# Native fp32 scores for the paired heads of a hybrid attention layer, with their copies and the output-weight split moved between engines

## Chip, cores and metric

The kernel runs on one core of a Trainium2 chip. The metric is device microseconds of one execution, the median over several runs. The engines are called PE (TensorE; PEld is its weight load), DVE (VectorE), ACT (ScalarE), POOL (GpSimd) and SP (SyncE, which issues the DMAs).

## What is computed

One decoder layer on x (512 tokens, width 1024), all fp32: a pre-norm and one input projection; eight latent-attention heads (0 to 7, query width 96); eight block-sparse heads (8 to 15, width 64, which with 512 tokens amount to causal attention with rotated queries and keys); the 16 head outputs together go through one output projection `w_out`, post-norm and residual; then a squared-ReLU MLP with the same norms. The part that matters here:

```python
mla_o = mla_attention(c_q, c_kv, k_r, ...)                      # heads 0 to 7
moba_o = moba_attention(rope(q), rope(k), v)                    # heads 8 to 15, scale 64 ** -0.5
mix = jnp.concatenate([mla_o..., moba_o...], axis=-1)
h = h + rms_norm(mix @ w_out[l], attn_post_g[l])
u = rms_norm(h, mlp_pre_g[l])
a = jnp.square(jax.nn.relu(u @ w_up[l]))
h = h + rms_norm(a @ w_down[l], mlp_post_g[l])
```

## The kernel before, in words

**Split products.** Most products are made at near-fp32 accuracy from three passes of the type fp32r: each operand is split into a high part (ACT, `hi_part`, L562) and a low part, the whole minus the high part (DVE, `lo_part`, L882; POOL for some pieces, L501), and PE makes high*high, high*low and low*high (`mm3`, L1329 to L1331). The weighted sums of values (`weighted`, L1556) are made in native fp32 with one matmul call per head and key tile, each of which stands as two records in the trace. Transposes are matmuls against an identity.

**Heads.** Queries stand in four tiles t of 128 tokens; tile t needs keys 0 to 128(t+1). Heads 0 to 7 are worked one by one. Heads 8 to 15 are worked in pairs m = 4 to 7 (`FIRST` = 4, `NP` = 8), one head in the upper and one in the lower 64 rows of PE's array. A turn m on PE is: scores of pair m for tiles 3, 2, 0 (`pair_scores`, L1497); what is left of the transposes of the last pair; transposes of the probabilities of head a = 2m-2 (`probs_T`, L1535); the weighted sums of pair m-2; scores of tile 1; the last transposes of a, those of head b = 2m-1; and, for m = 4 and 5, the transposes of keys and queries of pair m+2 (`k_prep` L1460, `q_prep` L1441). After the last turn come weighted sums of pair 6, transposes of head 14, one output tile of chunk 0 (`out_early(0)`, 12 products), transposes of head 15, one output tile of chunk 1 (`out_early(1)`), weighted sums of pair 7, then the other tiles of chunks 0 and 1 (72 products), then chunks 2 and 3.

**The other engines in a turn.** DVE takes row maxima (L996), ACT makes exponentials and their sums (L654), DVE inverts the sums (L1023), POOL multiplies the probabilities by them (`norm`, L508), PE transposes them into banks 3, 4 and 5, and ACT (`p_part`, L682) or DVE (L1045) copy these to SBUF, each bank having to be copied before it is used again (`p3_ready`, `p4_ready`, `p5_ready`). Queries and keys of a pair are split from their bank by ACT then DVE (`q_part`, `k_part`). Every engine works in the order written out by hand; semaphores tie them together. The scores of pair m wait for all exponentials of pair m-1 (`s_exp`).

**Output weights.** `w_out` comes in four chunks of 1 MB. SP loads chunks 0 and 1 early, chunk 2 once the split of chunk 0 is complete (`wo_ready` at 1), chunk 3 once that of chunk 1 is (`wo_ready` at 2). Chunks 0 and 1 are split in eight pieces of 512 columns, high part by ACT, low part by POOL (`out_piece`). `OUT_PIECES` and `PAIR_PIECES` say behind which turn each piece is made: piece 0 after head 6, piece 1 with turn 4, piece 2 with turn 5, pieces 3 and 4 with turn 6, 5 and 6 with turn 7, piece 7 after that. On POOL the pieces of a turn stand behind its norms, that is behind the eight `norm` calls of that turn. Chunks 2 and 3 (pieces 8 to 15) are split by ACT and DVE after the last weighted sum.

Of the kernel before, what the change touches and what calls it, by code (L numbers as in the profile page):

```python
# [23 lines left out]
P = 128  # L24
# [8 lines left out]
def build(nc, x, attn_pre_g, w_in, mla_q_norm_g, w_mla_q_up, mla_kv_norm_g, w_mla_kv_up, w_out,  # L33
# [42 lines left out]
    with ExitStack() as ctx:  # L76
# [126 lines left out]
        qT_full, qh, ql = sem("qT_full"), sem("qh"), sem("ql")  # L203
        kT_full, kh, kl = sem("kT_full"), sem("kh"), sem("kl")
        s_full, s_nb, s_exp = sem("s_full"), sem("s_nb"), sem("s_exp")
        s_ri, s_norm = sem("s_ri"), sem("s_norm")
# [36 lines left out]


        def by_head(w):
            return w[:, 0:HEADS * P].rearrange("p (h k c) -> p h k c", h=HEADS, k=2)
# [201 lines left out]
        def _(pool):  # L448
# [62 lines left out]
            for i in range(HEADS):  # L511
                for n in OUT_PIECES.get(i - 1, []):
# [33 lines left out]
        def _(act):  # L546
# [89 lines left out]
            def q_part(i):  # L636
                if prepared(i):
                    act.wait_ge(qT_full, preps(i))
                    if before(i) >= 0:
                        act.wait_ge(s_full, 3 * (before(i) + 1))  # L640
                    rows = QH if i < HEADS else P
                    hi_part(qT_hi[slot(i)][0:rows, :], ps[q_bank(i)][0:rows, :]).then_inc(qh, 1)

            def k_part(i):
                if prepared(i):
# [3 lines left out]
                    r0, rows = (NOPE * (i % 2), NOPE) if i < HEADS else (0, P)  # L649
                    hi_part(kT_hi[slot(i)][0:rows, :], ps[k_bank(i)][r0:r0 + rows, :]).then_inc(kh, 1)  # L650

# [59 lines left out]
            for i in range(1, HEADS - 1):  # L711
                if i >= 2:
                    p_part(i - 1, 0)
                if i <= 4:
                    k_part(i + 2)
                if i == 5:
                    o_part(0)
                for n in OUT_PIECES.get(i, []):
                    out_piece(n)
                if i >= 2:  # L720
                    p_part(i - 1, 2)
                exps(i + 1, S_ORDER[:1])
                if i == 6:
                    k_part(HEADS + 2)
                q_part(i + 2)
                exps(i + 1, S_ORDER[1:])
                if i in (4, 5):
                    k_part(i + 3)

            for m in range(FIRST, NP):  # L730
# [19 lines left out]
                for n in PAIR_PIECES[m]:  # L750
                    out_piece(n)
            p_part(NH - 2, 0)
            o_part(NP - 2)
            for n in PAIR_PIECES[NP]:
                out_piece(n)
            p_part(NH - 2, 2)
            p_part(NH - 1, 0)
# [115 lines left out]
        def _(dve):  # L873
# [151 lines left out]
            def q_part(i):  # L1025
                if prepared(i):
                    dve.wait_ge(qh, preps(i))
                    rows = QH if i < HEADS else P
                    s = slot(i)
                    lo_part(qT_lo[s][0:rows, :], ps[q_bank(i)][0:rows, :], qT_hi[s][0:rows, :]).then_inc(ql, 1)  # L1030

            def k_part(i):
                if prepared(i):
                    dve.wait_ge(kh, preps(i))
                    r0, rows = (NOPE * (i % 2), NOPE) if i < HEADS else (0, P)
                    s = slot(i)
                    lo_part(kT_lo[s][0:rows, :], ps[k_bank(i)][r0:r0 + rows, :], kT_hi[s][0:rows, :]).then_inc(kl, 1)

# [25 lines left out]
            def out_piece(n):  # L1064

                per = CW // PIECE
                c, w = n // per, slice(PIECE * (n % per), PIECE * (n % per) + PIECE)
                dve.wait_ge(wo_hi_ready, n + 1)
                last = lo_part(wo_lo[c - 2][:, w], raw[c % 2][:, w], wo_hi[c - 2][:, w])
                if n % per == per - 1:  # L1070
                    last.then_inc(wo_ready, 1)
# [18 lines left out]
            for m in range(FIRST, NP):  # L1090
# [235 lines left out]
        def _(pe):  # L1326
# [98 lines left out]
            def q_prep(i):  # L1425
                if prepared(i):
# [17 lines left out]
            def k_prep(i):  # L1444

                if i % 2 == 0 and i < NH:
                    b = k_bank(i)
                    if i in (2, 4):
                        pe.wait_ge(v_ready, NT + (3 if i == 2 else 4))
                    elif i > HEADS + 2:  # L1450
                        pe.wait_ge(p5_ready, i - 5)
                    elif i > 4:
                        pe.wait_ge(kl, i if i <= HEADS else preps(i) - 1)
                    if i < HEADS:
# [24 lines left out]
            def pair_scores(m, tiles):  # L1479

                s = slot(2 * m)
                if 3 in tiles:
                    pe.wait_ge(kl, preps(2 * m))
                    pe.wait_ge(ql, preps(2 * m))
                for t in tiles:
                    if t == 3:
                        pe.wait_ge(s_exp, 2 * NT * m)
                    if t == 2 and m == FIRST:
                        pe.wait_ge(kl, preps(HEADS + 2))
# [28 lines left out]
            def probs_T(i, tiles):  # L1518
                if tiles[0] == 0:
                    pe.wait_ge(s_norm, NT * (i + 1) + (1 if i >= HEADS and i % 2 == 0 else 0))  # L1520
                for k in tiles:
# [8 lines left out]
                    if k == 2 and i == HEADS - 2:  # L1530
                        pe.wait_ge(ql, preps(HEADS + 2))
                    if k == 2 and i in (HEADS - 1, HEADS + 1):
                        pe.wait_ge(kl, preps(i + 5))
                    for t in range(k, NT):
# [5 lines left out]
            def weighted(m, tiles):  # L1540

                if 0 in tiles:
# [3 lines left out]
                    if m in (FIRST - 1, FIRST):  # L1546
                        pe.wait_ge(ql, preps(HEADS + 4) + m - (FIRST - 1))
                for k in tiles:
# [52 lines left out]
            for m in range(FIRST, NP):  # L1601
# [23 lines left out]
            for c in range(2):  # L1625
                for t in range(1, NT):
                    if c == 0 and t == NT - 1:
                        pe.wait_ge(ol, NH // 2)
                    last = out_tile(t, c)
                last.then_inc(w_used, 1)  # L1630
            pe.wait_ge(wo_ready, NO)
# [123 lines left out]
```

## Time and profile before

| | |
|---|---|
| median of 3 runs | 566.77 us (565.98 to 567.16) |
| the profiled execution | 567.1 us, its span 565.3 us |
| PE busy | 550.5 us, 97% of the span |
| DVE, ACT, POOL busy | 391.9, 297.3, 95.4 us |
| mean granted TensorE clock | 0.998 |

Times inside the trace are microseconds from the start of the span. The profiled execution's own time is 1.8 us above its span. The input projection fills the span to about 100 us, the heads and pairs to about 188, the output projection to about 236, the MLP the rest.

### The profile page before, as it was taken

What the parts mean: (1) busy time and instruction counts of PE and PEld (TensorE: products, weight loads), DVE (VectorE), ACT (ScalarE), POOL (GpSimd) and SP (SyncE); (2) the same over time, 40 slices, a digit from 0 to 9 for tenths busy, and PEclk for the clock granted to TensorE, in tenths of its full rate; (3) what the DMA queues carried; (4) which work ended last, traced back from release to release, by engine and by line L of the source; (5) the groups of instructions that cost most, each with busy time, mean ns of one, the idle gap of its engine ahead of it and who ended that gap; (6) DMA issues with size and microseconds to landing.
All of it is one profiled execution on the core that took longest, in us unless ns stands there. A gap on an engine that the chain in (4) does not pass through costs nothing.

```text
span 565.3 us, 7927 instructions
## 1 busy us (share of the span) xinstructions
PE 550.5 (97%) x2776; PEld 457.7 (81%) x2776; DVE 391.9 (69%) x750; ACT 297.3 (53%) x624; POOL 95.4 (17%) x157
## 2 busy tenths in 40 slices
PE   7999999999999999999999999999999999999994
PEld 7988898877666788998888888888888888888883
DVE  5349563488875446457775776579868889787897
ACT  6563172688886354445335334435454657556461
POOL 1253210355779002200000000000000001000003
PEclk9999999999999999999999999999999999999999
DMA  8921522000002750078767888687984555606403
GB/s 293 375 84 57 176 85 75 0 2 2 0 2 78 277 188 18 26 294 301 272 225 277 273 272 288 226 282 278 346 301 173 215 181 193 217 14 215 150 0 149
DMA packets 41774, 97.23 MB, mean 172 GB/s; under 512 B 2192, under 2 KB 20368, under 8 KB 38416
## 3 DMA queue, kind: packets, MB, share of 16 engines
q1 hardware_dynamic: 41312, 96.32, 48.9%
q10 hardware_dynamic: 432, 0.53, 0.3%
q8 instruction: 17, 0.28, 0.2%
q14 instruction: 13, 0.11, 0.1%
HBM read 81.11 MB, written 15.73 MB: 171 GB/s over the span
## 4 chain that ended last, share of the span: by engine, by line
PE 93%; ACT 2%; DVE 2%; issue 1%; DMA 1%; POOLq 0%; DVEq 0%; POOL 0%; ACTq 0%
PE bank L1329 27%; PE bank L1331 27%; PE bank L1330 27%; PE bank L1357 4%; PE bank L1535 2%; PE bank L1556 2%; PE bank L1497 1%; ACT probs L654 1%; DVE bank L996 1%; DMA g_in<-in_attn_pre_g 1%; PE bank L1441 1%; PE bank L1335 1%; ACT pT L682 0%; DVE pT L1045 0%; PE bank L1396 0%
## 5 line engine op out<-in xcount | busy, mean ns | idle before, releaser
L1329 PE MATMUL bank<-uT_hi,w_hi 128*128 128x512 f32 (+1 forms) x280 | 104.1, 372 | 0.0
L1330 PE MATMUL bank<-uT_lo,w_hi 128*128 128x512 f32 (+1 forms) x280 | 103.8, 371 | 0.0
L1331 PE MATMUL bank<-uT_hi,w_lo 128*128 128x512 f32 (+1 forms) x280 | 103.8, 371 | 0.0
L1329 PE MATMUL bank<-w_hi,a_hi 128*128 128x512 f32 x224 | 87.2, 389 | 0.0
L1330 PE MATMUL bank<-w_lo,a_hi 128*128 128x512 f32 x224 | 87.1, 389 | 0.0
L1331 PE MATMUL bank<-w_hi,a_lo 128*128 128x512 f32 x224 | 87.1, 389 | 0.0
L885 DVE SCALAR_TENSOR_TENSOR w_lo<-w_raw,g_up,w_hi 128x256 fp32r<-128x256 f32 x128 | 52.1, 479 | 47.5 <-ACT w_hi L562 47.5
L562 ACT ACTIVATE w_hi<-w_raw,g_up 128x256 fp32r<-128x256 f32 x128 | 53.0, 496 | 44.8 <-PE bank L1331 25.0
L562 ACT ACTIVATE w_hi<-w_raw 128x1024 fp32r<-128x1024 f32 (+2 forms) x49 | 46.8, 1001 | 52.4 <-PE bank L1331 48.8
L882 DVE TENSOR_TENSOR w_lo<-w_raw,w_hi 128x1024 fp32r<-128x1024 f32 (+1 forms) x41 | 49.0, 1234 | 22.2 <-ACT w_hi L562 22.1
L1331 PEld LDWEIGHTS bank<-uT_hi,w_lo 128*128 128x128 f32 x280 | 52.7, 188 | 9.1
L1330 PEld LDWEIGHTS bank<-uT_lo,w_hi 128*128 128x128 f32 x280 | 52.7, 188 | 9.0
L1329 PEld LDWEIGHTS bank<-uT_hi,w_hi 128*128 128x128 f32 x280 | 52.7, 188 | 9.0
L508 POOL TENSOR_TENSOR probs<-probs,rs 128x512 f32<-128x512 f32 (+3 forms) x64 | 44.1, 723 | 54.1 <-DVE rs L1016 46.6
L1329 PE MATMUL bank<-w_hi,uT_hi 128*128 128x512 f32 x128 | 50.3, 393 | 0.0
L1331 PE MATMUL bank<-w_hi,uT_lo 128*128 128x512 f32 x128 | 49.9, 390 | 0.0
L1330 PE MATMUL bank<-w_lo,uT_hi 128*128 128x512 f32 x128 | 49.8, 389 | 0.0
L1329 PEld LDWEIGHTS bank<-w_hi,a_hi 128*128 128x128 f32 x224 | 42.0, 188 | 9.0 <-issue 0.4
L1331 PEld LDWEIGHTS bank<-w_hi,a_lo 128*128 128x128 f32 x224 | 42.0, 188 | 8.8
L1330 PEld LDWEIGHTS bank<-w_lo,a_hi 128*128 128x128 f32 x224 | 42.0, 188 | 8.8
L824 ACT ACTIVATE act_sb<-relu 128x512 f32 (+1 forms) x32 | 20.0, 624 | 51.1 <-DVE relu L1188 51.1
L538 POOL TENSOR_TENSOR relu<-relu,post_g 128x512 f32<-128x512 f32 x2 | 2.7, 1396 | 230.9 <-ACT junk_down L590 230.9
(163 smaller groups left out, 975.7 us busy)
## 6 DMA issues: line engine op xcount, KB each, us to landing
stage<-in_w_down SPq DMA_DIRECT2D x17, 1024.0 KB, 4.9
w_raw<-in_w_up SPq DMA_DIRECT2D x16, 1024.0 KB, 8.4
pair_sums<-stage SPq DMA_DIRECT2D x13, 1024.0 KB, 9.9
w_raw<-in_w_down SPq DMA_DIRECT2D x10, 1024.0 KB, 6.5
w_raw<-pair_sums SPq DMA_DIRECT2D x10, 1024.0 KB, 4.8
w_raw<-in_w_in SPq DMA_DIRECT2D x6, 1024.0 KB, 6.9
w_raw<-in_w_out SPq DMA_DIRECT2D x4, 1024.0 KB, 4.8
stage<-pair_sums SPq DMA_DIRECT2D x3, 1024.0 KB, 4.8
```

The lines of the kernel that those rows point to most:

```text
L508: nc.gpsimd.tensor_tensor(pr, pr, rs[:, i % 4, t:t + 1].to_broadcast([P, P * (t + 1)]), ALU.mult).then_inc(s_norm, 1)
L562: return nc.scalar.activation(out, whole, ACT.Copy, scale=scale)
L654: nc.scalar.activation(probs[i % 4][:, p_off(t):p_off(t) + n], ps[b][:, c:c + n], ACT.Exp, bias=nb[:, i % 4, t:t + 1], scale=-1.0, accum_o ...
L824: nc.scalar.activation(act_sb[:, bass.ds(i * 4 + tile, 1), :], relu[:, tile % 2:tile % 2 + 1, :], ACT.Square).then_inc(a_ready, 1)
L882: return nc.vector.tensor_tensor(out, whole, hi.bitcast(F32), ALU.subtract)
L885: return nc.vector.scalar_tensor_tensor(out=out, in0=whole, scalar=scale, in1=hi.bitcast(F32), op0=ALU.mult, op1=ALU.subtract)
L1329: nc.tensor.matmul(out, lh, rh, start=start, stop=False)
L1330: nc.tensor.matmul(out, lh, rl, start=False, stop=False)
L1331: return nc.tensor.matmul(out, ll, rh, start=False, stop=stop)
L1357: last = nc.tensor.matmul(ps[t][:, 0:CA], x[:, k, P * t:P * t + P], h[s][:, w], start=k == 0 and n == 0, stop=k == ND - 1 and n == 2)
L1535: last = nc.tensor.transpose(ps[b][:, c + P * (t - k):c + P * (t - k) + P], probs[i % 4][:, p_off(t) + P * k:p_off(t) + P * k + P], ident[ ...
L1556: last = nc.tensor.matmul(ps[6][r0:r0 + VD, P * k:TOP], v_sb[:, i // HEADS, k, vc], pT[i % 4][:, w], start=k == 0, stop=k == NT - 1)
```

## The change

- Queries and keys of heads 8 to 15 are copied whole, in fp32, from their bank to new tiles `mqT` and `mkT` by DVE alone (semaphores `mq_ready`, `mk_ready`); ACT has no part in them. The third copies of the four fp32r tiles go.
- `pair_scores` makes one native fp32 matmul call per head and tile where it made three fp32r ones.
- The third copy of the transposed probabilities (bank 5, 256 columns) of heads 6, 8, 10, 12 and 14 goes from ACT to DVE, right behind the last maxima of a turn.
- POOL makes only pieces 0 to 3 (one behind each turn 4 to 7); DVE makes pieces 4 to 7, behind the copies of head 15.
- On PE, the tile of chunk 0 is moved ahead of the last transposes and weighted sums but one; the early tile of chunk 1 goes, and in its place stand 12 products of chunk 0 (`SPARE`). All of chunk 1 comes after all of chunk 0.

```diff
-        for name, tiles in (("qT_hi", qT_hi), ("qT_lo", qT_lo), ("kT_hi", kT_hi), ("kT_lo", kT_lo)):
-            tiles.append(sb(f"{name}2", [P, S], F32R, stack=att))
+        mqT, mkT = [[sb(f"{n}{i}", [P, S], stack=att) for i in range(3)] for n in ("mqT", "mkT")]
...
         def ACT_COPIES(i, n):
-            return n == 0 or n == 2 and (i < HEADS or i % 2 == 0 or i in (HEADS - 1, HEADS + 1))
+            return n == 0 or n == 2 and (i < HEADS - 2 or i in (HEADS - 1, HEADS + 1))
...
-        OUT_PIECES = {6: [0]}
-        PAIR_PIECES = {4: [1], 5: [2], 6: [3, 4], 7: [5, 6], 8: [7]}
+        PAIR_PIECES = {4: [0], 5: [1], 6: [2], 7: [3], 8: [4, 5, 6, 7]}
...
@@ gpsimd @@
-            for n in PAIR_PIECES[NP]:
-                out_piece(n)
...
@@ scalar @@
-                pair_exps(m, [6])
-                p_part(a, 2)
-                pair_exps(m, [7])
+                pair_exps(m, [6, 7])
...
+            for n in PAIR_PIECES[NP]:
+                out_piece(n)
             p_part(NH - 2, 0)
             o_part(NP - 2)
-            for n in PAIR_PIECES[NP]:
-                out_piece(n)
-            p_part(NH - 2, 2)
             p_part(NH - 1, 0)
...
@@ vector @@
             def q_part(i):
-                if prepared(i):
+                if i >= HEADS:
+                    dve.wait_ge(qT_full, preps(i))
+                    if before(i) >= 0:
+                        dve.wait_ge(s_full, 3 * (before(i) + 1))
+                    nc.vector.tensor_copy(whole_q(i), ps[q_bank(i)][:, :]).then_inc(mq_ready, 1)
...
                 pair_maxes(m, [6, 7])
+                p_part(a, 2)
                 o_part(m - 2)
...
             p_part(NH - 2, 1)
+            p_part(NH - 2, 2)
             o_part(NP - 2)
             p_part(NH - 1, 1)
             p_part(NH - 1, 2)
+            dve.wait_ge(wo_ready, 1)
+            for n in PAIR_PIECES[NP]:
+                out_piece(n)
             o_part(NP - 1)
...
@@ tensor @@
-                    elif i == HEADS + 2:
-                        pe.wait_ge(ql, preps(HEADS))
+                    elif i == HEADS + 2:
+                        pe.wait_ge(mq_ready, 1)
...
-                    for n, (q, k) in enumerate(((qT_hi, kT_hi), (qT_hi, kT_lo), (qT_lo, kT_hi))):
-                        for h in range(2):
-                            b, c = PAIR_AT[t][h]
-                            r = slice(MOBA_D * h, MOBA_D * h + MOBA_D)
-                            last = nc.tensor.matmul(ps[b][:, c:c + w], q[s][r, tok], k[s][r, 0:w], start=n == 0, stop=n == 2)
-                            if n == 2 and t != 2:
-                                last.then_inc(s_full, 1)
+                    for h in range(2):
+                        b, c = PAIR_AT[t][h]
+                        r = slice(MOBA_D * h, MOBA_D * h + MOBA_D)
+                        last = nc.tensor.matmul(ps[b][:, c:c + w], whole_q(2 * m)[r, tok], whole_k(2 * m)[r, 0:w],
+                                                start=True, stop=True)
+                        if t != 2:
+                            last.then_inc(s_full, 1)
...
-            def out_early(c):
+            def out_ready(c):
 
                 pe.wait_ge(wo_ready, c + 1)
                 pe.wait_ge(s_exp, NT * NH)
                 pe.wait_ge(ol, 2 * (c + 1))
-                out_tile(0, c)
+
+            SPARE = ((1, 0), (3, 1))
...
+            out_ready(0)
+            out_tile(0, 0)
+            probs_T(NH - 2, PT_ORDER)
             weighted(NP - 2, range(NT))
-            probs_T(NH - 2, PT_ORDER)
-            out_early(0)
             probs_T(NH - 1, PT_ORDER)
-            out_early(1)
+            for t, b in SPARE:
+                for kk in range(2):
+                    out_rows(t, b, 0, kk)
             weighted(NP - 1, range(NT))
```

## Rows read from the trace of the kernel before

**Rows 1.** The page: the chain that ended last, by engine.

```profile
PE 93%; ACT 2%; DVE 2%; issue 1%; DMA 1%; POOLq 0%; DVEq 0%; POOL 0%; ACTq 0%
```

**Rows 2.** Timeline of PE, turns 4 to 7: start, us, what [idle before, releaser].

```profile
137.42 0.65 PE L1460 MATMUL bank<-ident,mk_nat 128*128 128x128 f32 x4 [0.32 <-DVE kT_lo L882]
...
142.11 0.50 PE L1497 MATMUL bank<-kT_hi,qT_hi 64*128 64x512 f32 x2 [0.93 <-ACT probs L654]
...
149.69 0.66 PE L1460 MATMUL bank<-ident,mk_nat 128*128 128x128 f32 x4 [0.25 <-ACT pT L682]
...
158.45 0.66 PE L1460 MATMUL bank<-ident,mk_nat 128*128 128x128 f32 x4 [0.62 <-ACT pT L682]
...
167.22 0.44 PE L1535 MATMUL bank<-ident,probs 128*128 128x128 f32 x2 [0.64 <-ACT pT L682]
...
174.87 0.44 PE L1535 MATMUL bank<-ident,probs 128*128 128x128 f32 x2 [0.20 <-ACT pT L682]
175.81 2.37 PE L1556 MATMUL bank<-pT,v_sb 128*64 128x512 f32 x16 [0.51 <-ACT pT L682]
```

**Rows 3.** Windows: us, PE, PEld, DVE, ACT, POOL busy, clock, DMA.

```profile
176.00:188.30 12.30, 12.30 (x77) 8.49 (x75) 2.38 (x4) 3.26 (x7) 6.46 (x8) 1.00 0.28 97
```

**Rows 4.** Timeline of PE: scores of pair 5 and what follows them.

```profile
150.71 0.50 PE L1497 MATMUL bank<-kT_hi,qT_hi 64*128 64x512 f32 x2
...
151.04 0.39 PE L1497 MATMUL bank<-kT_lo,qT_hi 64*128 64x512 f32 x2
...
151.27 0.40 PE L1497 MATMUL bank<-kT_hi,qT_lo 64*128 64x512 f32 x2
...
152.42 1.31 PE L1535 MATMUL bank<-ident,probs 128*128 128x128 f32 x10
...
155.97 0.39 PE L1497 MATMUL bank<-kT_hi,qT_hi 64*128 64x256 f32 x2
...
156.52 1.31 PE L1535 MATMUL bank<-ident,probs 128*128 128x128 f32 x10
```

**Rows 5.** Groups by form, 128 to 190 us: busy, mean ns, idle before.

```profile
L1045 DVE COPY pT<-bank 128x512 f32<-128x512 f32 x12 | 8.1, 676 | 5.9 <-PE bank L1535 5.9
...
L562 ACT ACTIVATE kT_hi<-bank 128x512 fp32r<-128x512 f32 x4 | 2.5, 632 | 0.0
```

**Rows 6.** Timeline of DVE at the end of turn 7.

```profile
174.80 0.17 DVE L1023 RECIPROCAL rs<-rs 128x3 f32<-128x3 f32 x1
...
175.54 0.40 DVE L1045 COPY pT<-bank 128x256 f32<-128x256 f32 x1
```

**Rows 7.** Timeline of POOL, turns 6 and 7: norms (L508) and pieces (L501).

```profile
167.33 3.48 POOL L508 TENSOR_TENSOR probs<-probs,rs 128x256 f32<-128x256 f32 x6 [1.35 <-DVE rs L1023]
170.77 2.52 POOL L501 TENSOR_TENSOR w_lo<-w_raw,w_hi 128x512 fp32r<-128x512 f32 x2
173.22 5.49 POOL L508 TENSOR_TENSOR probs<-probs,rs 128x512 f32<-128x512 f32 x8
```

**Rows 8.** Timeline of SP, PE and DVE: chunk loads, first product after weighting, late pieces.

```profile
172.08 10.77 SPq L342 DMA_DIRECT2D w_raw<-in_w_out  x2
...
188.26 0.50 PE L1329 MATMUL bank<-w_hi,uT_hi 128*128 128x512 f32 x1
...
189.62 4.90 DVE L882 TENSOR_TENSOR wo_lo<-w_raw,wo_hi 128x512 fp32r<-128x512 f32 x8
```

**Rows 9.** Windows at the end; PE at the start: timeline, groups 3:9.5 and 10.5:25.

```profile
558.30:562.80 4.50, 0.00 (x0) 0.00 (x0) 4.02 (x6) 0.72 (x2) 2.08 (x4) 1.00 0.31 118
562.80:565.30 2.50, 0.00 (x0) 0.00 (x0) 0.08 (x1) 0.00 (x0) 0.00 (x0) 0.50 0.54 210
...
5.85 1.76 PE L1357 MATMUL bank<-w_hi,uT_hi 128*128 128x416 f32 x4 [0.87 <-ACT w_hi L562]
...
L1357 PE MATMUL bank<-w_hi,uT_hi 128*128 128x416 f32 x4 | 1.8, 590 | 0.9 <-ACT w_hi L562 0.9
...
L1357 PE MATMUL bank<-w_hi,uT_hi 128*128 128x416 f32 x26 | 9.1, 351 | 0.0
```

More of the change, by code:

```diff
@@ L242, in before, with whole_q, whole_k @@
             return i - 2 if i < HEADS else SLOT_BEFORE.get(i, -1)
+        def whole_q(i):
+            return mqT[slot(i)][:, :]
+        def whole_k(i):
+            return mkT[slot(i)][:, :]
         def by_head(w):
@@ L511, in _ @@
             for i in range(HEADS):
-                for n in OUT_PIECES.get(i - 1, []):
-                    out_piece(n)
                 for n, t in enumerate(S_ORDER):
@@ L636, in q_part @@
             def q_part(i):
-                if prepared(i):
+                if i < HEADS:
                     act.wait_ge(qT_full, preps(i))
@@ L640, in q_part @@
                         act.wait_ge(s_full, 3 * (before(i) + 1))
-                    rows = QH if i < HEADS else P
-                    hi_part(qT_hi[slot(i)][0:rows, :], ps[q_bank(i)][0:rows, :]).then_inc(qh, 1)
+                    hi_part(qT_hi[slot(i)][0:QH, :], ps[q_bank(i)][0:QH, :]).then_inc(qh, 1)
             def k_part(i):
-                if prepared(i):
+                if i < HEADS:
                     act.wait_ge(kT_full, k_preps(i))
@@ L648, in k_part @@
                         act.wait_ge(s_full, 3 * (before(i) + 1))
-                    r0, rows = (NOPE * (i % 2), NOPE) if i < HEADS else (0, P)
-                    hi_part(kT_hi[slot(i)][0:rows, :], ps[k_bank(i)][r0:r0 + rows, :]).then_inc(kh, 1)
+                    r0 = NOPE * (i % 2)
+                    hi_part(kT_hi[slot(i)][0:NOPE, :], ps[k_bank(i)][r0:r0 + NOPE, :]).then_inc(kh, 1)
             def exp_tile(i, t, b, c):
@@ L717, in _ @@
                     o_part(0)
-                for n in OUT_PIECES.get(i, []):
-                    out_piece(n)
                 if i >= 2:
@@ L1025, in q_part @@
             def q_part(i):
-                if prepared(i):
+                if i >= HEADS:
[3 more added lines that the diff above has]
+                    nc.vector.tensor_copy(whole_q(i), ps[q_bank(i)][:, :]).then_inc(mq_ready, 1)
+                else:
                     dve.wait_ge(qh, preps(i))
-                    rows = QH if i < HEADS else P
                     s = slot(i)
-                    lo_part(qT_lo[s][0:rows, :], ps[q_bank(i)][0:rows, :], qT_hi[s][0:rows, :]).then_inc(ql, 1)
+                    lo_part(qT_lo[s][0:QH, :], ps[q_bank(i)][0:QH, :], qT_hi[s][0:QH, :]).then_inc(ql, 1)
             def k_part(i):
-                if prepared(i):
+                if i >= HEADS:
+                    dve.wait_ge(kT_full, k_preps(i))
+                    if before(i) >= 0:
+                        dve.wait_ge(s_full, 3 * (before(i) + 1))
+                    nc.vector.tensor_copy(whole_k(i), ps[k_bank(i)][:, :]).then_inc(mk_ready, 1)
+                else:
                     dve.wait_ge(kh, preps(i))
-                    r0, rows = (NOPE * (i % 2), NOPE) if i < HEADS else (0, P)
-                    s = slot(i)
-                    lo_part(kT_lo[s][0:rows, :], ps[k_bank(i)][r0:r0 + rows, :], kT_hi[s][0:rows, :]).then_inc(kl, 1)
+                    r0, s = NOPE * (i % 2), slot(i)
+                    lo_part(kT_lo[s][0:NOPE, :], ps[k_bank(i)][r0:r0 + NOPE, :], kT_hi[s][0:NOPE, :]).then_inc(kl, 1)
             def p_part(i, n):
@@ L1068, in out_piece @@
                 dve.wait_ge(wo_hi_ready, n + 1)
-                last = lo_part(wo_lo[c - 2][:, w], raw[c % 2][:, w], wo_hi[c - 2][:, w])
+                hi, lo = (w_hi[w_slot(OUT_CH[c])], w_lo[w_slot(OUT_CH[c])]) if c < 2 else (wo_hi[c - 2], wo_lo[c - 2])
+                last = lo_part(lo[:, w], raw[c % 2][:, w], hi[:, w])
                 if n % per == per - 1:
@@ L1451, in k_prep @@
                         pe.wait_ge(p5_ready, i - 5)
+                    elif i == HEADS + 2:
+                        pe.wait_ge(mk_ready, 1)
                     elif i > 4:
-                        pe.wait_ge(kl, i if i <= HEADS else preps(i) - 1)
+                        pe.wait_ge(kl, i)
                     if i < HEADS:
@@ L1479, in pair_scores @@
             def pair_scores(m, tiles):
-                s = slot(2 * m)
                 if 3 in tiles:
-                    pe.wait_ge(kl, preps(2 * m))
-                    pe.wait_ge(ql, preps(2 * m))
+                    pe.wait_ge(mk_ready, m - FIRST + 1)
+                    pe.wait_ge(mq_ready, m - FIRST + 1)
                 for t in tiles:
@@ L1617, in _ @@
                     probs_T(b, PT_ORDER[3:])
+            out_ready(0)
+            out_tile(0, 0)
+            probs_T(NH - 2, PT_ORDER)
             weighted(NP - 2, range(NT))
-            probs_T(NH - 2, PT_ORDER)
-            out_early(0)
             probs_T(NH - 1, PT_ORDER)
-            out_early(1)
+            for t, b in SPARE:
+                for kk in range(2):
+                    out_rows(t, b, 0, kk)
             weighted(NP - 1, range(NT))
[L1625 to L1630, printed above, removed]
+            for t in range(1, NT):
+                for b in range(2):
+                    if (t, b) not in SPARE:
+                        for kk in range(2):
+                            if t == NT - 1:
+                                pe.wait_ge(ol, NH // 2)
+                            last = out_rows(t, b, 0, kk)
+            last.then_inc(w_used, 1)
+            out_ready(1)
+            for t in range(NT):
+                last = out_tile(t, 1)
+            last.then_inc(w_used, 1)
             pe.wait_ge(wo_ready, NO)
```

10 lines of the change are left out of this document (5 added, 5 removed).

## The prediction

> **What bounds the kernel.** I read the chain of waits first: PE carries 93% of it [rows 1], so a microsecond saved on PE is a microsecond only where PE runs or waits on the chain. The change lies between about 137 and 205 us, so I read PE's timeline there and looked for the rows with idle time ahead. There are five of them before the last turn's exponentials are summed: 0.32, 0.93, 0.25, 0.62 and 0.64 us, together 2.76, and then 0.20 and 0.51 [rows 2]. All the rest is packed: PE alone sets the pace of a turn, with ACT as the engine it waits for in six of the seven. From 176.00 to 188.30 PE is busy for all of the 12.30 us [rows 3]. Last I read POOL, because the change makes PE wait for one of its products at a new place. POOL is far from busy over the whole kernel, but it is solidly filled in turn 7 [rows 7].
>
> **The scores.** Before, the first part of a pair's scores (tiles 3, 2, 0; 1024 columns for each head) takes 152.42 - 150.71 = 1.71 us, tile 1 (256 columns) 156.52 - 155.97 = 0.55, together 2.26 [rows 4]. A pass of 512 columns for both heads starts 0.23 after the last one (151.04 to 151.27), so the two heads, in two halves of the array's rows, run at the same time. No row shows native fp32 with the array halved by rows. The nearest one is the weighted sum: native fp32, two heads in two halves of the array's columns, the same 1280 columns for each head, 2.37 us (the row at 175.81 [rows 2]). From it the first part would be 2.37 * 1024/1280 = 1.90 and tile 1 0.47 plus a start of some 0.11 (the first pass, 150.71 to 151.04, is that much longer than the next), 0.58. That is 0.19 + 0.03 = 0.22 more a pair, 0.9 for four. Bounds: no change in cost (the weighted sum in one piece is within 0.11 of 2.26), and, if the halves take turns, 2.1 more a pair (rival B). I take 0.9, by the nearest row. The gain of going from three passes to one call is thus nothing: a native call costs about what three passes do.
>
> **The copies.** ACT loses kT_hi and qT_hi of four pairs, 0.63 each [rows 5]. DVE makes one copy of 0.68 where it made a low part of 0.69 (the row of the 512-column copy stands for it), and no longer waits for ACT first. So the wait of 0.32 for kT_lo goes, and in front of the first pair ACT makes no kT_hi and qT_hi between the exponentials of head 7, for which PE waits 0.93. DVE must still take the maxima and make both copies before pair 4 starts, so I take 1.0 of these 1.25 as gained. Bounds 0.7 and 1.25.
>
> **The bank-5 copy.** ACT made it between the last two exponentials of a turn, and PE waited for it: 0.25, 0.62, 0.64, 0.20. DVE now makes it right behind the last maxima. DVE's own copy of this size takes 0.40 [rows 6]. Followed through each turn: in turn 4 the copy still ends about when PE wants the bank, 0.1 gained; in turn 5 0.5 gained; in turn 6 the bank is free in time, but the scores of pair 7 wait for the last exponential of pair 6, 0.2 gained net. Late next there is ACT's last exponential. Queued on DVE behind the copy are the low part of the head outputs and the reciprocals of the last sums, for which POOL waits: they come 0.35 later than the gain of PE would have them.
> Sum of gains at the reciprocal of turn 7 (174.80 before [rows 6]): 1.0 + 0.1 + 0.5 + 0.2 - 0.9 - 0.35 = 0.55. Bounds -0.3 and 2.8 (all five waits gone, scores and copy at nothing).
>
> **The end of the pairs decides.** Piece 3, the last one of chunk 0, was made by POOL with turn 6: norms end and the two pieces 3 and 4 start at 170.77, and SP loads chunk 2 at 172.08, once piece 3 is through [rows 7, 8]. It now stands behind all norms of turn 7. In turn 6 the six norms behind the reciprocal take 170.77 - 167.33 = 3.44, a piece 2.52 / 2 = 1.26 [rows 7]. From the reciprocal at 174.80, 0.25 until POOL starts (the reciprocal's 0.17 and a little), 3.44 and 1.26: 179.75 with nothing gained, 179.2 with the 0.55. The earlier norms are no longer held up by a second piece (POOL started those of turn 7 only at 173.22), but those behind the last reciprocal are not early for it.
> PE is through with turn 7 at 174.87 + 0.44 = 175.3, or about 174.2 with its gains. Its next instruction is now the tile of chunk 0, which waits for `wo_ready` at 1. Behind this wait are queued the transposes of head 14 and the weighted sums of pair 6, which need only norms long done or done 1.3 earlier, and which before filled exactly this time. So PE stands still for about 5.0 us, from 174.2 to 179.2.
> The work behind is what it was: 24 products, twice ten transposes, two weighted sums. Before it ran from 175.81 to 188.26, 12.45 us. So 179.2 + 12.45 = 191.65, against 188.26: **3.4 us later**. Without any gain it would be 3.9.
>
> **What lies beside other work.** DVE's pieces 4 to 7 take 4 * 0.69 = 2.8 behind the copies of head 15; chunk 1 is wanted only behind the 24 remaining products of chunk 0, some 5.5 us after the last weighted sum, so they are hidden. Chunk 2 loads 7 us later (179 for 172), chunk 3 at about 190 for 182.4. A load took under 6 us; with 4.9 for DVE's eight late pieces [rows 8] the split is done near 200. PE wants it after 72 products, at 0.23 each 16.6 us, at 208. Hidden, by 8 us. The next loads of SP (x again, the first of `w_up`) stand behind chunk 3 and move with the rest; if that cover went, it would cost what chunk 3's 1 MB takes, some 3 us. POOL's last pieces, behind its norms, cost nothing before and nothing now. ACT's pieces 4 to 7 fall in PE's pause.
>
> **Sum.** 567.1 + 3.4 = 570.5 for the profiled execution. The median of before is 0.3 lower, 566.8, so **570.2** for the median. A measurement of this kernel can tell about 0.2%, 1.1 us, from no change.
>
> **Rivals.**
> A. *The pause lowers PE's clock.* [...] The pause I forecast is 5.0. At the start, PE took up work at 5.85 after a wait of 0.9; the same form of product took 590 ns up to 9.5 and 351 from 10.5 on [rows 9]. [...] Such a stretch costs about half of it, 2.0: 572.2 (1 to 3 us by when it falls). [...] Chance 0.34.
> [...]
> B. *The halves take turns in native fp32.* For: no row has this form. Against: the weighted sums overlap in native fp32, the scores overlap by rows in fp32r. Price 2.1 a pair, 8.5 for four, all ahead of the reciprocal: 579. Chance 0.05.
> C. *Not slower.* The place is the reciprocal of turn 7, which sets POOL's piece 3. If the turns get so much shorter that it comes 2.8 earlier, the loss is under 1.1; from 3.9 on it is none. All five waits gone with scores and copy at nothing give 2.76: 568.0. Were the native call also quicker than the three passes by 0.1 a pair: 567.6. For: ACT loses 0.63 twice a pair and 0.4 in each turn, and ACT is what PE waits for. Against: with those gone, PE's own work fills the turn, and POOL's norms follow the reciprocal in any case. Chance 0.08.
> D. *The change does less than it says,* the calls being run as fp32r all the same. The new tiles are plain fp32 like the weighted sums', so I give this nothing of its own; it would leave 3.4 - 0.9 = 2.5.
>
> **Chances.** Forecast (3.4 later, clock up) 0.45, 569.4 to 570.9 from the bounds above; A 0.34, 571.2 to 573.4; B 0.05; C 0.08; 0.08 for a loss in between or beyond by a late load. The range 569.0 to 573.8 takes in the first two. Slower by over 0.2% (over 567.9): 0.90; same 0.07; faster 0.03.
>
> **What would show it.** Right: PE idle some 5 us ahead of the first product of the output projection (L1329's first row behind turn 7), released by POOL's w_lo (L501), which ends near 179; the waits for ACT at L1460 and L1535 gone or under 0.2; the first part of the scores near 1.9 us with two records a call; ACT without kT_hi of pairs; 24 products and weighted sums packed behind. Wrong: a PE that goes on without a wait at about 175 (C), scores of 3 to 4 us (B), a granted clock under 1.00 between 175 and 190 (A). My sum is wrong in size if the reciprocal of turn 7 is off 174.3 by more than a microsecond.

## The result, and the profile after

| | before | changed |
|---|---|---|
| median (6 runs each) | 566.78 us | **572.52 us** (571.84 to 573.8) |
| ratio, 95% interval | | 1.0100 (1.0087 to 1.0114) |
| profiled execution, its span | 567.1, 565.3 us | 571.84, 570.0 us |
| mean granted clock | 0.998 | 0.99, in every one of the 6 runs |

The change is 5.7 us slower. That is inside the range of 569.0 to 573.8, but not at its point: it is rival A, forecast at 572.2, and not the likeliest case of 570.2. The profiled execution of the changed kernel was the fastest of its six, and that of the kernel before was 0.3 above its median, so the traces differ by less (571.84 - 567.1 = 4.7) than the medians do.

The chain of waits of the changed kernel (its page) answers to [rows 1]: PE has grown from 93% to 95%, and POOL, at nothing before, has 1%, which is its time under PE's pause.

```profile
PE 95%; POOL 1%; DVE 1%; DMA 1%; issue 0%; ACT 0%; POOLq 0%; DVEq 0%; ACTq 0%
```

PE's timeline in the turns (as in [rows 2] and [rows 4]):

```profile
132.29 0.60 PE L1469 MATMUL bank<-ident,mk_nat 128*128 128x128 f32 x4
...
136.26 0.60 PE L1469 MATMUL bank<-ident,mk_nat 128*128 128x128 f32 x4
...
140.23 2.00 PE L1504 MATMUL bank<-mkT,mqT 64*128 64x512 f32 x12 [0.27 <-DVE mqT L1023]
...
147.86 0.66 PE L1469 MATMUL bank<-ident,mk_nat 128*128 128x128 f32 x4
...
149.04 2.00 PE L1504 MATMUL bank<-mkT,mqT 64*128 64x512 f32 x12
150.97 1.31 PE L1543 MATMUL bank<-ident,probs 128*128 128x128 f32 x10
...
154.51 0.70 PE L1504 MATMUL bank<-mkT,mqT 64*128 64x256 f32 x4
155.15 1.31 PE L1543 MATMUL bank<-ident,probs 128*128 128x128 f32 x10
...
165.53 2.00 PE L1504 MATMUL bank<-mkT,mqT 64*128 64x512 f32 x12
```

All waits for ACT of 0.2 us and more are gone; one of 0.27 for DVE's copy of the queries is new. The first part of the scores takes 150.97 - 149.04 = 1.93 us (1.71 before), tile 1 0.64 (0.55 before), and the 12 and 4 records stand for two a call: it is native fp32, with both heads at the same time (one record of each head starts at 149.04, and 0.70 us later both are through).

A caution in reading the two traces side by side: at 132.29 the changed kernel does what the kernel before did at 132.97, and PE's instructions up to there are the same. Most of the difference stands already near the start, where PE's first products are slow for some microseconds in both traces (590 ns each for 351 later before [rows 9], 589 for 350 in the changed kernel's), and for less long in the changed kernel's: the first quick one starts at 10.04 before and at 9.41 after. It is not a gain of the change: the two traces of one kernel run twice reach this row at 132.65 and 133.14. So 0.68 us of every gain read off the clock of the trace is the two executions' own start. Below, stretches are counted from this row (the first transposes of keys in native form, L1460 before, L1469 after), and end at the first product behind the last weighted sum: 188.26 - 132.97 = 55.29 before, 193.02 - 132.29 = 60.73 after, **5.44 more**.

What follows turn 7, on PE, then DVE's reciprocal of turn 7 and what POOL does meanwhile (as in [rows 6, 7, 8]):

```profile
171.80 1.47 PE L1543 MATMUL bank<-ident,probs 128*128 128x128 f32 x10
178.28 0.79 PE L1336 MATMUL bank<-w_hi,uT_hi 128*128 128x512 f32 x1 [5.01 <-POOL w_lo L506]
178.87 0.63 PE L1337 MATMUL bank<-w_lo,uT_hi 128*128 128x512 f32 x1
...
183.21 1.25 PE L1543 MATMUL bank<-ident,probs 128*128 128x128 f32 x10
184.40 2.38 PE L1564 MATMUL bank<-pT,v_sb 128*64 128x512 f32 x16
...
190.72 2.37 PE L1564 MATMUL bank<-pT,v_sb 128*64 128x512 f32 x16
193.02 0.50 PE L1336 MATMUL bank<-w_hi,uT_hi 128*128 128x512 f32 x1
```

```profile
173.29 0.17 DVE L1016 RECIPROCAL rs<-rs 128x3 f32<-128x3 f32 x1
...
170.42 2.04 POOL L513 TENSOR_TENSOR probs<-probs,rs 128x512 f32<-128x512 f32 x2
173.53 3.47 POOL L513 TENSOR_TENSOR probs<-probs,rs 128x256 f32<-128x256 f32 x6 [1.07 <-DVE rs L1016]
176.96 1.26 POOL L506 TENSOR_TENSOR w_lo<-w_raw,w_hi 128x512 fp32r<-128x512 f32 x1
```

PE stands still for 5.01 us, released by POOL's piece 3. Then it works at another pace: 0.43 from product to product where it was 0.23. Windows of the same kernel (us, PE, PEld, DVE, ACT, POOL busy, clock, DMA):

```profile
174.00:175.00 1.00, 0.00 (x0) 0.00 (x0) 0.43 (x3) 1.00 (x3) 1.00 (x3) 1.00 0.00 0
175.00:176.00 1.00, 0.00 (x0) 0.00 (x0) 0.00 (x0) 1.00 (x3) 1.00 (x3) 0.98 0.00 0
176.00:177.00 1.00, 0.00 (x0) 0.00 (x0) 0.00 (x0) 0.25 (x1) 1.00 (x3) 0.50 0.00 0
...
178.30:183.20 4.90, 4.90 (x12) 3.81 (x13) 0.00 (x0) 0.00 (x0) 0.00 (x0) 0.54 0.57 215
```

The granted clock falls to 0.50 at 175.96, 2.7 us after PE's last transpose (171.80 + 1.47), and is up again near 182.8. The work behind the pause takes 193.02 - 178.28 = 14.74 us, where the forecast had 12.45 from [rows 2, 8], 2.29 more. Not all of this is the clock's: with the pause filled and the clock up (experiment 2) the same work takes 191.36 - 178.67 = 12.69, so 2.05 is for the clock and 0.24 for the new order.

### The profile page after: what moved, and what is told of

Its sections match the earlier page's. It is cut to its first block, busy times and chain, and to the rows that moved or that the text cites. A ratio compares the mean times of both kernels' runs of the same rounds, so it can differ in the third digit from the quotient of the medians.

```text
span 570.0 us, 7856 instructions
## 1 busy us (share of the span) xinstructions
PE 553.6 (97%) x2744; PEld 456.7 (80%) x2744; DVE 395.5 (69%) x759; ACT 293.4 (51%) x611; POOL 91.0 (16%) x153
## 4 chain that ended last, share of the span: by engine, by line
PE 95%; POOL 1%; DVE 1%; DMA 1%; issue 0%; ACT 0%; POOLq 0%; DVEq 0%; ACTq 0%
PE bank L1336 27%; PE bank L1337 27%; PE bank L1338 27%; PE bank L1364 3%; PE bank L1543 3%; PE bank L1564 3%; PE bank L1504 2%; POOL probs L513 1%; PE bank L1448 1%; DMA g_in<-in_attn_pre_g 1%; PE bank L1342 1%; DVE bank L989 0%; PE bank L1469 0%; PE bank L1403 0%; POOL w_lo L506 0%
## 5 line engine op out<-in xcount | busy, mean ns | idle before, releaser
L875 DVE TENSOR_TENSOR w_lo<-w_raw,w_hi 128x1024 fp32r<-128x1024 f32 (+2 forms) x45 | 51.4, 1185 | 22.4 <-ACT w_hi L561 22.2
L652 ACT ACTIVATE probs<-bank,nb 128x512 f32<-128x512 f32 (+3 forms) x64 | 33.3, 529 | 17.2 <-DVE nb L989 16.7
```

The costliest lines, as they stand in the source:

```text
L652: nc.scalar.activation(probs[i % 4][:, p_off(t):p_off(t) + n], ps[b][:, c:c + n], ACT.Exp, bias=nb[:, i % 4, t:t + 1], scale=-1.0, accum_o ...
L875: return nc.vector.tensor_tensor(out, whole, hi.bitcast(F32), ALU.subtract)
```

## Experiments

In all, ten kernels in twelve runs. The medians drift by up to a microsecond from one chip session to the next (before: 566.78 to 567.8), so ratios are taken against the kernel before in the same session. The stretch defined above, read in each trace, tells finer differences than the medians do; in the two kernels run twice it came out within 0.01 us. Each is read from one execution, so where the clock falls inside the stretch it holds for a fall as that execution had it.

| kernel | median, before beside it | ratio (95%) | stretch, against 55.29 |
|---|---|---|---|
| changed | 572.52, 566.78 | 1.0100 (1.0087 to 1.0114) | 60.73, +5.44 |
| scores' side alone | 566.29, 567.2 | 0.9983 (0.9974 to 0.9992) | 53.86, -1.43 |
| pieces and PE's end alone | 574.09, 567.2 | 1.0114 (1.0097 to 1.0131) | 61.90, +6.61 |
| pause filled | 570.34, 567.2 | 1.0063 (1.0049 to 1.0076) | 58.68, +3.39 |
| pause part filled | 572.36, 567.8 | 1.0076 (1.0062 to 1.0090) | 61.11, +5.82 |
| PE's order back | 567.65, 567.8 | 0.9997 (0.9987 to 1.0006) | 55.11, -0.18 |
| piece 3 in turn 6 | 565.69, 567.2 | 0.9979 (0.9970 to 0.9988) | 53.59, -1.70 |
| the same, again | 565.46, 567.45 | 0.9966 (0.9953 to 0.9978) | 53.60, -1.69 |
| bank-5 copy alone | 566.07, 567.8 | 0.9968 (0.9956 to 0.9980) | 54.25, -1.04 |
| the same, again | 566.57, 567.45 | 0.9983 (0.9974 to 0.9992) | 54.26, -1.03 |
| whole scores alone | 566.6, 567.8 | 0.9980 (0.9970 to 0.9989) | 54.38, -0.91 |
| split scores, piece 3 in turn 6 | 566.22, 567.45 | 0.9976 (0.9967 to 0.9985) | 53.95, -1.34 |
| one-pass scores | 563.46, 567.45 | 0.9929 (0.9916 to 0.9943) | 51.24, -4.05 |

**1. Which half of the change costs.** The scores' side alone is the changed kernel with this undone:

```diff
-        PAIR_PIECES = {4: [0], 5: [1], 6: [2], 7: [3], 8: [4, 5, 6, 7]}
+        OUT_PIECES = {6: [0]}
+        PAIR_PIECES = {4: [1], 5: [2], 6: [3, 4], 7: [5, 6], 8: [7]}
...
-            out_ready(0)
-            out_tile(0, 0)
-            probs_T(NH - 2, PT_ORDER)
             weighted(NP - 2, range(NT))
+            probs_T(NH - 2, PT_ORDER)
+            out_early(0)
```

> The changed kernel with pieces 0 to 7, their order on ACT and POOL, and PE's order behind turn 7 all as before; native scores, DVE copies and the bank-5 copies on DVE stay. Theory (the loss is PE's pause for piece 3 and the clock it costs; the scores' side is a gain): no pause over 1 us, clock 1.00, some 1.5 us faster than before, 565.3. Rival (native scores cost the time): slower than before, 568 or more.

The pieces and PE's end alone is the mirror of it: the kernel before, with those lines as in the change.

> The kernel before with only the pieces and PE's order behind turn 7 as in the change; the scores stay in fp32r, split by ACT and DVE. Theory: piece 3 ends near 179.8, PE pauses 4.5 us from 175.3, the clock falls for some 6.8 us and costs 2.1: 3.9 + 2.1 more than before, 572.8. Rival (native scores cost the time): about 567.

Measured: 0.9 us faster (566.29 against 567.2), and 6.9 slower (574.09). The second kernel's timeline of PE has all its old waits and the pause:

```profile
142.54 0.50 PE L1492 MATMUL bank<-kT_hi,qT_hi 64*128 64x512 f32 x2 [0.93 <-ACT probs L647]
...
158.86 0.66 PE L1455 MATMUL bank<-ident,mk_nat 128*128 128x128 f32 x4 [0.63 <-ACT pT L675]
...
175.27 0.44 PE L1530 MATMUL bank<-ident,probs 128*128 128x128 f32 x2 [0.19 <-ACT pT L675]
180.18 0.80 PE L1324 MATMUL bank<-w_hi,uT_hi 128*128 128x512 f32 x1 [4.47 <-POOL w_lo L500]
```

and its row of waits `PE bank L1324 <- POOL w_lo L500: 4.5, 1, 4.5`. So the loss is whole without any native score, and the scores' side is a gain. Both parts add up: in the stretch -1.43 + 6.61 = 5.18, where both together are 5.44. The theory stands, the rival (native scores cost the time) falls. The size was a little off: 1.5 us was expected of the first, 0.9 measured by the medians (0.5 to 1.5 by the interval), and 6.0 of the second, 6.9 measured. In its profiled execution the work behind the pause took 15.13 us, 0.39 more than in the changed kernel: the clock's share is not the same every time.

**2. The clock's share.** PE's pause is filled with small bf16 products whose results are never used:

```diff
+            pe.wait_ge(s_exp, NT * NH)
+            warm(80)
             out_ready(0)
             out_tile(0, 0)
```

> The changed kernel with 80 small bf16 products of the identity (results overwritten, never used) in PE's pause, some 4.4 us of the 5.0, behind the wait for the last exponentials. Theory (the fall of the clock costs 2.1 us of work behind the pause): clock stays 1.00 to the end, the first product of chunk 0 still starts within 0.3 us of 178.3, time 2.1 less than the change, 570.4. Rival (the clock costs nothing because the engines behind it set the pace): 572.5.

```profile
171.91 1.74 PE L1543 MATMUL bank<-ident,probs 128*128 128x128 f32 x12
173.61 4.64 PE L1393 MATMUL bank<-ident_b 128*128 128x128 bf16 x80
178.67 0.50 PE L1336 MATMUL bank<-w_hi,uT_hi 128*128 128x512 f32 x1 [0.42 <-POOL w_lo L506]
```

```profile
173.60:178.30 4.70, 4.65 (x81) 4.47 (x80) 1.21 (x5) 3.03 (x6) 4.38 (x7) 1.00 0.02 3
178.30:183.20 4.90, 4.53 (x24) 3.52 (x26) 0.49 (x1) 0.59 (x1) 0.32 (x1) 1.00 0.60 214
```

The first fence is PE's timeline of this kernel, the second its windows (us, PE, PEld, DVE, ACT, POOL busy, clock, DMA). The product of chunk 0 starts where it did (178.67 - 132.68 = 45.99 from the common row, against 178.28 - 132.29 = 45.99 in the changed kernel), the clock stays at 1.00, and in the same 4.9 us 24 products and transposes get done where there were 12. The stretch is 2.05 shorter than the change's (60.73 to 58.68). By ratios, 1.0063 for 1.0100, the gain is 2.1; by the medians, each against the kernel before beside it, it is 2.6. So the clock costs 2.1 to 2.6 us and the waiting itself the rest, 3.4 in the stretch, net of what the scores' side gains.

Then 24 such products instead of 80:

> As the filled pause, with 24 small products (results unused) in place of 80: PE works 1.4 us more and then stands still for about 3.5. Theory that any pause of over 2.7 us (the time from PE's last transpose to the fall in the changed kernel) lowers the clock: as the change, 572.5, clock 0.99. Rival, that more than the pause's length counts, and a pause under 4 us is let pass in some or all runs: 570.4, clock 1.00.

In the profiled execution PE stood still for 3.54 us and the clock fell all the same, in its windows 2.1 us after its last small product (173.91 + 1.51 = 175.42 to near 177.5):

```profile
177.00:177.50 0.50, 0.00 (x0) 0.00 (x0) 0.00 (x0) 0.00 (x0) 0.50 (x1) 1.00 0.00 0
177.50:179.00 1.50, 0.04 (x1) 0.04 (x1) 0.00 (x0) 0.00 (x0) 1.41 (x2) 0.51 0.00 0
```

But that execution was the slowest of the five (572.97), and the five do not agree. Their mean granted clocks are 0.99, 0.993, 0.995, 0.993 and 0.995, where the changed kernel has 0.99 six times. A mean of 0.995 over 570.5 us leaves at most 2 * 0.0055 * 570.5 = 6.3 us at the lower level (an estimate, with the rounding). In the traces the fall in the pause lasts 6.8 us, and the ends of the 14 traces have 2.0 to 5.3 us at the lower level. So in two of the five the fall in the pause was shorter, or did not come. The median of 572.36 looks like the first theory's, but the kernel before beside it was slow too (567.8): the ratio is 1.0076, between 1.0063 with the pause filled and 1.0100 for the change. Neither side holds as written: a pause of 3.5 us does not lower the clock in the same way every time. The pieces alone, with a pause of 4.5 us, have one such execution as well, clock 0.995 and 572.29 us, against 0.99 to 0.992 and 573.03 to 574.53 for the other four.

The ends of the kernels show the same. There the clock falls after PE's last instruction, but not after a fixed time. One kernel run twice (piece 3 in turn 6) ends its work on PE at 556.40 and at 556.74. Windows of its two traces, first and second run:

```profile
556.40:558.40 2.00, 0.00 (x1) 0.00 (x0) 1.93 (x3) 0.72 (x2) 1.03 (x3) 1.00 0.00 0
558.40:559.40 1.00, 0.00 (x0) 0.00 (x0) 0.78 (x2) 0.00 (x0) 0.92 (x2) 0.68 0.03 10
...
556.70:561.70 5.00, 0.04 (x1) 0.00 (x0) 4.12 (x6) 0.72 (x2) 2.18 (x4) 1.00 0.29 113
561.70:562.20 0.50, 0.00 (x0) 0.00 (x0) 0.00 (x0) 0.00 (x0) 0.00 (x0) 0.63 1.05 410
```

A mean of 0.68 over 1.00 us puts the first fall at 558.76, 2.4 us after PE's last instruction, and 0.63 over 0.50 us puts the second at 561.83, 5.1 us after it. Over the 14 traces of this document the time goes from 2.1 (the changed kernel, PE's order back, bank-5 copy alone) to 5.3 (whole scores alone), with 4.6 in the kernel before. What decides it in one execution stays open; the next experiment has a pause short enough that the clock stays up.

**3. The order on PE.** Pieces stay as in the change; PE's order is put back:

```diff
-            out_ready(0)
-            out_tile(0, 0)
-            probs_T(NH - 2, PT_ORDER)
             weighted(NP - 2, range(NT))
+            probs_T(NH - 2, PT_ORDER)
+            out_ready(0)
+            out_tile(0, 0)
```

> The changed kernel with its pieces as they are (piece 3 still behind POOL's norms of turn 7), but on PE the weighted sums of pair 6 and the transposes of head 14 are put back ahead of the wait for piece 3. Theory: 3.6 us of work fill the pause, which shrinks from 5.0 to about 1.4, and the clock stays at 1.00: 3.6 + 2.1 less than the change, 0.2 us more or less than before. Rival (the place of piece 3 costs in any order, for the loads and pieces behind it): still 2 us or more over before.

```profile
174.72 2.38 PE L1564 MATMUL bank<-pT,v_sb 128*64 128x512 f32 x16 [0.43 <-ACT pT L680]
177.03 1.31 PE L1543 MATMUL bank<-ident,probs 128*128 128x128 f32 x10
179.31 0.50 PE L1336 MATMUL bank<-w_hi,uT_hi 128*128 128x512 f32 x1 [0.98 <-POOL w_lo L506]
```

5.6 us come back in the stretch (60.73 to 55.11) and the kernel is even with the one before (0.9997): 3.6 us of work now fill the pause, 1.0 of it is left, 0.43 goes to another wait, and the clock stayed at 1.00 through it. The theory stands and the rival falls: the late piece itself, with all the loads behind it, costs nothing further.

**4. The place of piece 3.** One piece earlier on POOL, the change's order on PE:

```diff
-        PAIR_PIECES = {4: [0], 5: [1], 6: [2], 7: [3], 8: [4, 5, 6, 7]}
+        PAIR_PIECES = {4: [0], 5: [1], 6: [2, 3], 7: [], 8: [4, 5, 6, 7]}
```

> The changed kernel with piece 3 made in turn 6 (behind piece 2) and none in turn 7; all else as in the change. Theory: wo_ready at 1 comes near 172, PE goes on without a pause at 173.3, clock 1.00; the 5.0 of the pause and 2.1 of the clock go: 7.2 less than the change, 565.3, faster than before by 1.5. Rival (POOL's norms of turn 7, held up by the second piece, make a new wait at the transposes of head 14): 1 to 2 us less of it back, 566.5 to 567.5.

> The same kernel as the run with piece 3 in turn 6, again beside the two above: 1.5 us faster than before.

Both runs are faster than before, by 1.5 and 2.0 us (0.9979 and 0.9966), and 7.1 us less in the stretch than the change, where 7.2 was expected. POOL is now filled without a gap from turn 6's last norms to turn 7's:

```profile
169.53 2.51 POOL L506 TENSOR_TENSOR w_lo<-w_raw,w_hi 128x512 fp32r<-128x512 f32 x2
172.00 5.47 POOL L513 TENSOR_TENSOR probs<-probs,rs 128x512 f32<-128x512 f32 x8
```

and PE has no wait behind turn 7 at all: the tile of chunk 0 stands in front of the transposes and covers even the 0.5 us that PE waited before the weighted sums [rows 2]. The rival, a new wait for the norms of turn 7, did not come. One number in a table of the kernel decides between 1% slower and 0.2 to 0.3% faster.

**5. Where the gain of the scores' side comes from.** The bank-5 copy alone, in the kernel before:

```diff
-            return n == 0 or n == 2 and (i < HEADS or i % 2 == 0 or i in (HEADS - 1, HEADS + 1))
+            return n == 0 or n == 2 and (i < HEADS - 2 or i in (HEADS - 1, HEADS + 1))
...
-                pair_exps(m, [6])
-                p_part(a, 2)
-                pair_exps(m, [7])
+                pair_exps(m, [6, 7])
```

> The kernel before with only the 256-column copy of heads 6, 8, 10, 12 and 14 moved from ACT to DVE, behind the last maxima. Theory: PE's waits for ACT of 0.25, 0.62, 0.64 and 0.20 shrink to under 0.2 each, of which 0.5 to 1.0 us stays at the end: 0.1 to 0.2% faster. Rival (the waits were the queues' own and return elsewhere, as DVE's reciprocals come later): no gain.

> The same kernel as the run with the bank-5 copy alone, again beside the run with piece 3 in turn 6: its trace gained 1.0 us where that one gained 1.7, so by the traces it is the slower of the two by 0.7; by the medians so far it is even with it.

Gains of 0.32% and 0.17% by the medians, 1.04 us in the stretch. In its timeline the waits of 0.25, 0.62, 0.64 and 0.20 are gone, and one of 0.47 stands ahead of pair 7, for ACT's last exponential:

```profile
166.68 0.50 PE L1496 MATMUL bank<-kT_hi,qT_hi 64*128 64x512 f32 x2 [0.47 <-ACT probs L654]
```

Next, whole scores alone: the first kernel of experiment 1 with the bank-5 copies back on ACT, between the last two exponentials.

> The run of the scores' side alone, with the bank-5 copies back on ACT: only native scores and DVE's whole copies of queries and keys differ from before. Theory: 1.2 us gained ahead of pair 4 (the waits of 0.32 and 0.93), 0.3 lost to each pair's dearer scores, of which PE's waits for the bank-5 copy take up part: 0.3 to 0.8 us faster than before. Rival (the native calls are the gain): as fast as with the bank-5 copies moved too, 0.9 faster.

0.9 us in the stretch, 0.2% (1.1 us) by the ratio: somewhat more than the 0.3 to 0.8 expected. By the medians it can't be told from the run with the bank-5 copies moved too (0.9980 and 0.9983), which is the rival's figure; by the stretch it is behind that run by 0.5 (53.86 and 54.38). That the native calls themselves are the gain does not follow from it: they take 2.57 us a pair where the three passes take 2.26, and the waits ahead of pair 4 have gone from 1.25 to 0.27. The waits for ACT's bank-5 copy have shrunk to 0.20 each even without moving it. The two gains are therefore not additive (1.04 and 0.91 alone, 1.43 together): each shortens the same waits for ACT's copy.

Last, the price of native scores against split ones with everything else equal: the kernel before with the bank-5 copy on DVE, piece 3 in turn 6 and the change's order on PE.

> The kernel before with the bank-5 copies on DVE, piece 3 in turn 6 and the change's order behind turn 7; scores and their operands stay split in fp32r. Against the run with piece 3 in turn 6 and native scores this prices the native scores and whole copies by themselves. Theory: the waits of 0.32 and 0.93 stay, four pairs' scores are 0.3 cheaper each: even within 0.3 us of that run, 565.7 to 566. Rival (native scores are worth a microsecond or more): 567.

53.95 against 53.59 with native scores: native scores and whole copies are worth 0.36 us in the stretch. By the medians, 566.22 and 565.46 in the same session, 0.8, with intervals that overlap (0.9967 to 0.9985, 0.9953 to 0.9978). So they are worth a few tenths, a little more than the 0.3 that was expected at most, and no full microsecond is shown. With split scores PE's waits of 0.32, 0.93 and 0.48 stay in the turns, 1.46 more than the 0.27 with native scores, and this outweighs the cheaper passes (4 * 0.31 = 1.24).

**6. Does PE set the pace of a turn now?** The run of experiment 4 with its whole queries and keys in fp32r, one pass; the two low passes are left out.

```diff
-        mqT, mkT = [[sb(f"{n}{i}", [P, S], stack=att) for i in range(3)] for n in ("mqT", "mkT")]
+        mqT, mkT = [[sb(f"{n}{i}", [P, S], F32R, stack=att) for i in range(3)] for n in ("mqT", "mkT")]
```

> The run with piece 3 in turn 6, its whole queries and keys written as fp32r and multiplied in one fp32r pass: the two low passes are left out, so scores are only coarse. It takes 1.2 us off PE in each pair's first part and 0.35 off tile 1. Theory (PE's own work now fills a turn, so what PE sheds is gained until DVE and POOL set the pace): 2 to 4 us faster than that run, 562 to 564, with waits back on PE. Rival (DVE, now with both copies, sets the pace already): under 1 us faster.

2.35 us less in the stretch and 2.0 in the median, for the some 6 us that PE sheds by the expectation's prices. That is the low end of the 2 to 4 expected; the rival, under 1 us, falls. What PE sheds is gained in part, and then other engines are the bound:

```profile
165.04 0.73 PE L1504 MATMUL bank<-mkT,mqT 64*128 64x512 f32 x6 [0.88 <-ACT probs L652]
166.68 1.09 PE L1543 MATMUL bank<-ident,probs 128*128 128x128 f32 x8 [0.91 <-POOL probs L513]
```

So with native scores PE is the bound of the turns, with some 0.6 us a turn (2.35 over four) between it and the others.

**The best version** of those run, with scores at full accuracy, is the one of experiment 4, faster than both kernels: 565.5 to 565.7 us.

## Why the prediction came out as it did

- *Scores.* The form no row showed, native fp32 with the array halved by rows, costs 1.93 + 0.64 = 2.57 a pair: 0.31 more than the three passes, where 0.22 was taken from the weighted sums. Of the 0.09 missed a pair, 0.03 is in the first part and 0.06 in tile 1. What makes it up, no run shows. That heads run at the same time was right, rival B out.
- *Copies.* 1.0 of the waits of 1.25 were taken as gained ahead of pair 4. Measured from the common row: (142.11 - 132.97) - (140.23 - 132.29) = 1.20, with the remaining 0.27 on DVE.
- *Bank-5 copy.* From the start of pair 4 to that of pair 7 the changed kernel takes 165.53 - 140.23 = 25.30, before 167.77 - 142.11 = 25.66: 0.36 net. The sum had 0.8 of gains less three pairs at 0.22, 0.14. The last exponential, named as what is late next, is what PE waits for in the run with the copy alone.
- *The reciprocal of turn 7* came at 173.29, 1.51 earlier in the trace and 0.83 from the common row, for a forecast of 0.55: inside the bounds.
- *The pause.* POOL's 0.24 + 3.47 + 1.26 behind the reciprocal give 178.26; the first product started at 178.28. The pause was 5.01, forecast 5.0. From the common row PE was through with turn 7 1.36 us earlier than before (175.31 to 173.27, less 0.68) and the reciprocal came 0.83 earlier, for forecasts of 1.1 and 0.55. The difference is the same, so the pause is 0.5 longer than the 4.5 of the pieces alone, as forecast. This was the mechanism of the whole result: a wait put in front of work that had covered it, not the wait's own lateness, as experiment 3 shows.
- *The clock.* This is the step that failed. The likeliest case had the clock up through a pause of 5.0 us. The clock fell after 2.7, with six runs of six at 0.99. The kernel before shows one time from last work to fall, 4.6 us at its end (558.24 to 562.8, as in [rows 9]); the ends of the 14 traces have it at 2.1 to 5.3, so this one is near the long end, and a time read once says little about the next. The price of 2.0 in rival A takes the slow first products of the kernel for some 4 us at the lower level, of which half is lost. No run shows this: the profile has the granted clock at 1.00 where the products took 590 ns as well as behind it, where they took 351 (windows below this list), and 351 for 590 is a loss of 0.4 and not of a half. What the runs showed in its place is a clock at 0.50 for 6.8 us, 4.5 of it with PE at work, at a cost of 2.1 to 2.6 us. That 2.0 comes near it is luck.
- *Rival C, not slower.* All its waits did go, yet the reciprocal gained 0.8 and not 2.8: PE's own work filled the turns, as its counter-argument said.
- *Hidden work.* The pieces 4 to 7 on DVE, the later loads of chunks 2 and 3 and those behind them cost nothing: the stretch's 5.44 is, to 0.06, the span's 570.0 - 565.3 = 4.7 plus the 0.68 of the start, so next to nothing is lost or found behind 193 us.
- *The bounds.* The forecast's 569.4 to 570.9 does not come out of its own bounds: gains of -0.3 to 2.8 at the reciprocal give losses of 4.2 to 1.1, that is 571.0 to 567.9. The stated range of 569.0 to 573.8 was wide enough for the measured time all the same.

Windows of the kernel before, among its slow first products and behind them (columns as above, the clock third from the end):

```profile
6.00:8.00 2.00, 2.00 (x6) 1.92 (x7) 1.08 (x2) 1.12 (x3) 0.00 (x0) 1.00 1.04 339
...
10.00:12.00 2.00, 2.00 (x13) 1.97 (x12) 2.00 (x4) 2.00 (x5) 0.00 (x0) 1.00 1.05 403
```

Forecast of the parts: 3.4 for the waiting and 2.0 for the clock, 5.4 together; measured 3.39 and 2.05 in the stretch, 5.44 together, 5.7 in the median. That 3.4 was met to 0.01 is luck: the first product came 0.24 earlier than forecast (45.99 from the common row against 179.2 - 132.97 = 46.23), and the work behind it took 0.24 longer.

## What to carry over

When a step is moved ahead of others on an in-order engine, look at what its wait needs on the slowest and fullest queue, and at which work had filled that time: moving the wait one step costs the fill, not just the lateness. A pause of a few microseconds on PE should be priced twice, for itself and for the lowered clock behind it (for the 5.01 us here, 58.68 - 55.11 = 3.6 in the stretch and 2.1 to 2.6), and an idle time seen once before a fall is one case out of a spread (2.1 to 5.3 us here), not a threshold: look at several traces, and at the granted clock of every run and not only of the profiled one. Two edits that each remove a wait for the same engine need not add up: here 1.04 and 0.91 us alone made 1.43 together.

## What was unexpected in the hardware

- The time from PE's last instruction to the fall of the clock is not fixed. In mid-kernel it was 2.7 us (the change, and the pieces alone) and 2.1 (pause part filled). At the kernels' ends it was 2.1 to 5.3 us over 14 traces, 4.6 in the kernel before (557.85 + 0.39 to 562.8), and 2.4 and 5.1 in two runs of one kernel. A pause of 1.0 us with one of 0.43 shortly ahead of it left the clock at 1.00, and so did 80 small bf16 products of 128 columns in the pause. It was down for 6.8 us in the traces of both the change and the part-filled pause, so there the shorter pause (3.54 us) left more work at the lower level than the longer one (5.01): its stretch is 61.11, against 58.68 with the pause filled, 2.4 us, and 60.73 for the longer, 2.1.
- Native fp32 matmuls of two heads in the two row halves of the array overlap as the weighted sums in its column halves do: 1.93 us for 1024 columns of each head, in scores and sums alike with a record of each head starting within 0.02 us (at 149.04 in the changed kernel, at 175.81 in the one before). Taking turns would have cost some 2 us more a pair (an estimate, from the 2.37 us that the weighted sums take for the same columns with both heads at once); 0.31 was measured.
